# An expert stage with four row buffers each way, gathers four experts ahead, and down products one expert behind

## The reference

```python
def run_block(args):
    idx, e, w = args
    xb = x_pad[idx]
    hb = jax.nn.silu(xb @ w_gate[e]) * (xb @ w_up[e])
    return (hb @ w_down[e]) * w[:, None]
```

## Time and profile before

| | us |
|---|---|
| runs of the kernel, median of 3 | 1197.54 (1194.24 to 1198.41) |
| the profiled execution | 1196.28 |
| its span, first to last instruction | 1194.5 |
| mean granted clock of TensorE | 0.916 of full |

### The profile page before, as it was taken

How to read it: one execution, slowest core, us unless ns; L and a number is a source line. 1 busy time by engine, 2 the same in 40 slices (tenths; PEclk the granted TensorE clock), 3 DMA queues, 4 the chain that set the end, 5 groups by cost and what they waited for, 6 DMA issues and landing times.

```text
span 1194.5 us, 12870 instructions
## 1 busy us (share of the span) xinstructions
PE 1012.9 (85%) x4516; PEld 669.6 (56%) x4516; DVE 435.5 (36%) x952; ACT 297.3 (25%) x481; POOL 206.0 (17%) x376
## 2 busy tenths in 40 slices
PE   6699899999989979999999999758676768777596
PEld 6478677677867756666666644624333334333242
DVE  5595457339337632622232112321111111111443
ACT  3223432433433243311211100111111111111232
POOL 0131411330250121000000000033333333332000
PEclk9999899989979978999999999579888898888798
DMA  5221032022003022422222070616888888987401
GB/s 199 88 71 36 1 123 71 1 88 88 18 0 123 0 80 79 197 103 80 79 79 79 3 297 35 282 12 260 355 346 366 348 357 329 370 354 276 165 28 43
DMA packets 29071, 176.36 MB, mean 148 GB/s; under 512 B 11836, under 2 KB 12220, under 8 KB 22768
## 3 DMA queue, kind: packets, MB, share of 16 engines
q1 hardware_dynamic: 23600, 167.41, 36.1%
q0 software_dynamic: 5440, 8.54, 1.9%
HBM read 171.59 MB, written 12.71 MB: 154 GB/s over the span
## 4 chain that ended last, share of the span: by engine, by line
PE 55%; issue 22%; DVE 9%; POOL 6%; DMA 5%; ACT 2%; POOLq 1%; DVEq 0%; SPq 0%; ACTq 0%
PE bank L753 52%; DVE arena L1231 2%; DMA expert_rows<-mT,sidx 2%; POOL mT L1585 2%; DVE low_parts L1164 2%; POOL takes_wait L1577 2%; DMA mT<-normed,gidx 1%; DVE arena L1271 1%; DMA arena<-in_w_branch 1%; POOL expert_rows L1594 1%; PE bank L973 1%; PE bank L845 1%; DVE hT_parts L1159 0%; PE bank L781 0%; DMA x_sb<-in_x 0%
## 5 line engine op out<-in xcount | busy, mean ns | idle before, releaser
L753 PE MATMUL bank<-arena 128*128 128x64 f32 (+7 forms) x624 | 188.0, 454 | 23.1 <-DVE arena L1255 8.9
L753 PE MATMUL bank<-arena,yT 128*64 128x256 f32 (+1 forms) x1280 | 188.7, 452 | 12.7 <-ACT yT L703 11.8
L753 PE MATMUL bank<-mT_parts,low_parts 128*128 128x512 f32 x448 | 178.2, 398 | 0.0
L753 PEld LDWEIGHTS bank<-arena 128*128 128x128 f32 (+1 forms) x624 | 109.7, 217 | 97.6 <-issue 70.3
L753 PE MATMUL bank<-mT_parts,x_parts 128*128 128x512 f32 x320 | 138.7, 433 | 17.2 <-DVE low_parts L1164 13.5
L753 PEld LDWEIGHTS bank<-arena,yT 128*64 128x64 f32 x1280 | 93.3, 144 | 101.2 <-issue 49.3
L753 PE MATMUL bank<-hT_parts,x_parts 128*128 128x512 f32 x320 | 128.7, 402 | 0.0
L1164 DVE TENSOR_TENSOR low_parts<-arena,x_parts 128x1024 fp32r<-128x1024 f32 (+1 forms) x44 | 62.3, 1416 | 148.2 <-ACT x_parts L567 118.4
L753 PEld LDWEIGHTS bank<-mT_parts,low_parts 128*128 128x128 f32 x448 | 85.2, 190 | 20.0
L1022 PE MATMUL bank<-cst,mT 128*128 128x128 f32 x128 | 25.6, 333 | 74.2 <-DMA mT<-normed,gidx 74.2
L753 PE MATMUL bank<-yT,arena 128*128 128x512 f32 x192 | 86.3, 592 | 0.0
(11 more groups left out here) (227 smaller groups left out, 1209.2 us busy)
## 6 DMA issues: line engine op xcount, KB each, us to landing
arena<-in_w_expert SPq DMA_DIRECT2D x32, 3072.0 KB
arena<-in_w_cm SPq DMA_DIRECT2D x32, 512.0 KB, 3.6
arena<-in_w_gate SPq DMA_DIRECT2D x8, 1536.0 KB, 6.5
arena<-in_w_tm SPq DMA_DIRECT2D x4, 1536.0 KB, 6.7
arena<-in_w_branch SPq DMA_DIRECT2D x8, 768.0 KB, 7.9
x_sb<-in_x SPq DMA_DIRECT2D x8, 512.0 KB, 5.5
arena<-in_w_out SPq DMA_DIRECT2D x1, 4096.0 KB, 12.1
arena<-in_w_pg SPq DMA_DIRECT2D x2, 2048.0 KB, 9.5
```

Of the source, the lines that this page charges most:

```text
L753: return pe.matmul(out, lhsT, rhs, start=start, stop=stop)
```

## The change

- There are four gathered-row buffers and four scattered-row buffers (`ROWS = 4`) in place of two and two, each with its own semaphore. The memset ahead of the stage covers four row buffers, 2048 columns in place of 1024. VectorE's code and SyncE's are as before.
- GpSimd gathers the first four blocks at once; afterwards gather n + 4 is issued once block n is turned, still ahead of the wait for the scaled result of n and scatter n in the same queue. The indices are read by the indirect DMA straight from `table`: the copies, their waits and `take_wait` are gone from the main path. The loops of GpSimd and ScalarE are straight-line code.
- TensorE's step n is now up(n + 1), turning of the hidden block of n, turning of the rows of n + 2, down(n); up(0) and the turning of block 1 stand ahead of step 0. ScalarE's is sigmoid(n + 1), hidden copy(n), scaling(n).
- A weight buffer is still released by down(n), which now stands behind up(n + 1).

```diff
+ROWS = 4
...
-        xr = [mflat[:, b * 512:(b + 1) * 512] for b in range(2)]
-        yr = [mflat[:, (2 + b) * 512:(3 + b) * 512] for b in range(2)]
+        xr = [mflat[:, b * 512:(b + 1) * 512] for b in range(ROWS)]
+        yr = [mflat[:, (ROWS + b) * 512:(ROWS + b + 1) * 512] for b in range(ROWS)]
...
-            def scale_rows(n, b2, scattered):
+            def scale_rows(n, b2, slot, scattered):
                 act.wait_ge(down_done, n + 1)
-                act.wait_ge(rows_scattered[b2], scattered)
-                act.activation(yr[b2], Y[b2][:, :], ACT.Copy, scale=table_w(n)).then_inc(y_scaled, 1)
+                if scattered is not None:
+                    act.wait_ge(rows_scattered[slot], scattered)
+                act.activation(yr[slot], Y[b2][:, :], ACT.Copy, scale=table_w(n)).then_inc(y_scaled, 1)
             act.wait_ge(table_loaded, 32)
             act.wait_ge(routed, 2)
             n_over = act.value_load(ctl[0:1, 0:1], min_val=0, max_val=MAX_OVER)
-            with act.Fori(0, NEXP // RING) as i:
-                for b in range(RING):
-                    gate_sigmoid(RING * i + b, b % 2)
-                    hidden_copy(RING * i + b, b % 2)
-                    scale_rows(RING * i + b, b % 2, (1 + 2 * i + b // 2) * 16)
-            for b in range(2):
+            gate_sigmoid(0, 0)
+            for n in range(NEXP):
+                if n + 1 < NEXP:
+                    gate_sigmoid(n + 1, (n + 1) % 2)
+                hidden_copy(n, n % 2)
+                scale_rows(n, n % 2, n % ROWS, n // ROWS * 16 if n >= ROWS else None)
...
+            pe.wait_ge(we_loaded[0], 16)
+            up(0, 0, we[0], nothing)
+            turn_block(1, 1, rows_gathered[1], 16)
+
+            def expert_step(n, i, b, first=False, y_unused=False, last_one=False, before_last=False):
                 b2, other = b % 2, (b + 1) % 2
-                pe.wait_ge(we_loaded[b], (i + 1) * 16)
-                up(n, b2, we[b], nothing if gu_unused else lambda: pe.wait_ge(h_swished, n - 1))
                 if not last_one:
-                    turn_block(n + 1, other, rows_gathered[other], (2 * i + (b + 1) // 2 + 1) * 16)
+                    pe.wait_ge(we_loaded[(b + 1) % RING], (i + 1 + (b + 1) // RING) * 16)
+                    up(n + 1, other, we[(b + 1) % RING],
+                       nothing if first else lambda: pe.wait_ge(h_swished, n))
                 turn_hidden(n, b2)
-                down(n, b2, we[b], nothing if gu_unused else lambda: pe.wait_ge(y_scaled, n - 1))
+                if not last_one and not before_last:
+                    turn_block(n + 2, (b + 2) % ROWS, rows_gathered[(b + 2) % ROWS], (i + (b + 2) // ROWS + 1) * 16)
+                down(n, b2, we[b], nothing if y_unused else lambda: pe.wait_ge(y_scaled, n - 1))
             for b in range(RING):
-                expert_step(b, 0, b, gu_unused=b < 2)
+                expert_step(b, 0, b, first=b == 0, y_unused=b < 2)
...
-            pool.memset(mflat[:, 0:D], 0.0).then_inc(ready, 1)
+            pool.memset(mflat[:, 0:ROWS * 512], 0.0).then_inc(ready, 1)
...
-            def gather(b2, col, done, count):
-
-                take_wait(0)
-                pool.tensor_copy(gidx[:, b2:b2 + 1, :], table[:, bass.ds(col, 1), 0:2]).then_inc(idx_copied, 1)
-                pool.wait_ge(idx_copied, count + 1)
-                take_wait(1)
-                pool.indirect_dma_start(out=xr[b2], out_offset=None, in_=normed_halves,
-                                        in_offset=bass.IndirectOffsetOnAxis(ap=gidx[:, b2, 0:1], axis=0),
+            def gather_rows(slot, token_halves, done):
+
+                pool.indirect_dma_start(out=xr[slot], out_offset=None, in_=normed_halves,
+                                        in_offset=bass.IndirectOffsetOnAxis(ap=token_halves, axis=0),
                                         bounds_check=2 * SEQ - 1, oob_is_err=False).then_inc(done, 16)
-            def scatter(b2, col, done, count):
-                take_wait(0)
-                pool.tensor_copy(sidx[:, b2:b2 + 1, :], table[:, bass.ds(col, 1), 0:2]).then_inc(idx_copied, 1)
-                pool.wait_ge(idx_copied, count + 1)
-                take_wait(1)
+            def scatter_rows(slot, row_halves, done):
+
                 pool.indirect_dma_start(out=expert_halves,
-                                        out_offset=bass.IndirectOffsetOnAxis(ap=sidx[:, b2, 1:2], axis=0),
-                                        in_=yr[b2], in_offset=None, bounds_check=4 * SEQ - 1,
+                                        out_offset=bass.IndirectOffsetOnAxis(ap=row_halves, axis=0),
+                                        in_=yr[slot], in_offset=None, bounds_check=4 * SEQ - 1,
                                         oob_is_err=False).then_inc(done, 16)
-            gather(0, 0, rows_gathered[0], 0)
-            gather(1, 1, rows_gathered[1], 1)
+            for n in range(ROWS):
+                gather_rows(n, table[:, n, 0:1], rows_gathered[n])
             pool.wait_ge(routed, 2)
             n_over = pool.value_load(ctl[0:1, 0:1], min_val=0, max_val=MAX_OVER)
-            def serve(n, b2, gathers, scattered):
-
-                if gathers is not None:
+            for n in range(NEXP):
+                slot = n % ROWS
+                if n + ROWS < NEXP:
                     pool.wait_ge(rows_turned, n + 1)
-                    pool.wait_ge(rows_gathered[b2], gathers)
-                    gather(b2, n + 2, rows_gathered[b2], 2 + 2 * n)
+                    gather_rows(slot, table[:, n + ROWS, 0:1], rows_gathered[slot])
                 pool.wait_ge(y_scaled, n + 1)
-                pool.wait_ge(rows_scattered[b2], scattered)
-                scatter(b2, n, rows_scattered[b2], NEXP + n if gathers is None else 3 + 2 * n)
-
-            with pool.Fori(0, NEXP // RING - 1) as i:
-                for b in range(RING):
-                    serve(RING * i + b, b % 2, (2 * i + b // 2 + 1) * 16, (1 + 2 * i + b // 2) * 16)
-            for n in range(NEXP - RING, NEXP):
-                serve(n, n % 2, (n // 2 + 1) * 16 if n + 2 < NEXP else None, (1 + n // 2) * 16)
-            for b in range(2):
-                pool.wait_ge(rows_gathered[b], NEXP // 2 * 16)
+                scatter_rows(slot, table[:, n, 1:2], rows_scattered[slot])
```

More of the change, by code:

```diff
@@ L399, in build @@
         idx_copied = sem("idx_copied")
-        rows_gathered = [sem("rows_gathered0"), sem("rows_gathered1")]
+        blank_stored = sem("blank_stored")
+        rows_gathered = [sem(f"rows_gathered{b}") for b in range(ROWS)]
         rows_turned = sem("rows_turned")
@@ L410, in build @@
         y_scaled = sem("y_scaled")
-        rows_scattered = [sem("rows_scattered0"), sem("rows_scattered1")]
+        rows_scattered = [sem(f"rows_scattered{b}") for b in range(ROWS)]
         ov_w = sem("ov_w")
@@ L433, in build @@
         TM_AFTER, TM_TILE_AT = 4, 10
-        SCATTERED = (1 + NEXP // 2) * 16
+        SCATTERED = NEXP // ROWS * 16
         CM_ORDER = 8
@@ L713, in _ @@
             n_over = act.value_load(ctl[0:1, 0:1], min_val=0, max_val=MAX_OVER)
-            with act.Fori(0, NEXP // RING) as i:
-                for b in range(RING):
-                    gate_sigmoid(RING * i + b, b % 2)
-                    hidden_copy(RING * i + b, b % 2)
-                    scale_rows(RING * i + b, b % 2, (1 + 2 * i + b // 2) * 16)
-            for b in range(2):
+            gate_sigmoid(0, 0)
[4 more added lines that the diff above has]
+                scale_rows(n, n % 2, n % ROWS, n // ROWS * 16 if n >= ROWS else None)
+            for b in range(ROWS):
                 act.wait_ge(rows_scattered[b], SCATTERED)
@@ L725, in _ @@
                         hidden_copy(NEXP + j, 0)
-                        scale_rows(NEXP + j, 0, SCATTERED + j * 16)
+                        scale_rows(NEXP + j, 0, 0, SCATTERED + j * 16)
             for t in range(T):
@@ L1013, in _, with turn_block @@
                 ple(t)
-            def turn_block(n, b2, gathered, value, first=False):
+            def turn_block(n, slot, gathered, value, first=False):
                 pe.wait_ge(gathered, value)
@@ L1021, in turn_block @@
                 for k in range(KD // 2):
-                    last = pe.transpose(TR[:, k * P:(k + 1) * P], xr[b2][:, k * P:(k + 1) * P], ident)
+                    last = pe.transpose(TR[:, k * P:(k + 1) * P], xr[slot][:, k * P:(k + 1) * P], ident)
                 last.then_inc(rows_turned, 1)
@@ L1525, in _ @@
                 pool.dma_start(table_dram.rearrange("(j b) w -> j b w", b=NBLK)[slots], blank[slots, :, :])\
-                    .then_inc(rows_scattered[half], 16)
-            for half in range(2):
-                pool.wait_ge(rows_scattered[half], 16)
+                    .then_inc(blank_stored, 16)
+            pool.wait_ge(blank_stored, 32)
             pool.wait_ge(if_projected, T)
@@ L1616, in _ @@
-            for n in range(NEXP - RING, NEXP):
```

(21 more changed lines are left out.)

3 lines of the change are left out of this document (1 added, 2 removed).

## The result

The changed kernel takes 1154.97 us (median of 4 runs, 1151.8 to 1157.76) against 1196.51 us for the kernel before. The ratio is 0.9653, with a 95% interval of 0.9622 to 0.9684: 3.5% faster. The forecast was 1154.

What follows compares the result with a forecast made beforehand. The bound was taken as a loop: late gather, no buffer release, dry weight queue. The stage's end moving from 1108.25 to 1066.9 (41.4 us) plus 0.5 bookkeeping, off 1196.3, gave 1154 us; range 1142 to 1168.

Steps and rivals of the forecast that it cites:

- DMA bounds after the change, at 8.1 us an expert: Expert stage: loads, gathers and scatters, 3.41 MB an expert, set the pace at 8.1 us, above TensorE's own work.
- The start, 3.8 us lost: Start of the expert stage: up(1) now precedes down(0), so the weight stream begins at 820.2 us, 3.8 us later.
- the 0.5 us for GpSimd's bookkeeping: Gathers and last scatter: without index copies, GpSimd's issue work shrinks by 0.5 us at each end, bounds 0 and 1.15.
- TensorE's floor, 6.5 us: Expert stage: TensorE's own work at full clock, with its small gaps covered by the new order, takes 6.5 us an expert.
- Rows at 9.0 us an expert beside 24 KB packets: Expert stage: row transfers advance packet for packet with weights, so a scatter with a gather needs 9.0 us an expert.
- rival A: Expert stage: no gather limit, weights alone set the pace; 50.7 us off, 1146 us, or 1140 at 7.9 a load; chance 0.18.
- One dry spell of 2.5 us at 951: Expert stage, step 16: the weight queue runs dry from 951.3 to 953.8 us, and the gathers catch up meanwhile.
- Rival D, the clock: Expert stage: short TensorE stops in every expert lower its clock; slower, about 1214 us at 65% low-clock work; chance 0.05.
- Rival C, an HBM limit near 358 GB/s: Expert stage: HBM sustains only some 357 GB/s, 9.5 us a load; 11.5 us off, 1185 us; chance 0.05.

Runs made afterwards that it cites:

- e8: The changed kernel with 28 of the 32 expert weight loads cut from 24 to 20 KB a partition; 1119.47 us, ratio 0.9353.
- e4: The changed kernel with each expert's weights loaded by two DMAs (16 KB and 8 KB a partition) instead of one; 1153.44 us, ratio 0.9644.
- e1: The changed kernel with two row buffers each way instead of four, so gathers run two experts ahead; 1363.78 us, ratio 1.1391.

## Why the prediction was right, point by point

- **DMA bounds after the change, at 8.1 us an expert.** Right, and e8 with e4 shows it: 35.2 us for 14.7 MB less, with 34.6 expected. From the first full window to the end the share is about 1.0 at 417 GB/s on average.
- **The start, 3.8 us lost.** Right: 4.0 (S 130.2 against 126.2), with the first release at 820.1 us (820.2 forecast). Of the 0.5 us for GpSimd's bookkeeping some 0.4 are seen: the last scatter starts 0.77 us after ScalarE's end, where it started 1.20 us after it before.
- **TensorE's floor, 6.5 us.** Too high, at no cost: with everything at hand the step is 6.02 us (817.96 to 823.98).
- **Rows at 9.0 us an expert beside 24 KB packets.** The mechanism is right: the first wait for rows inside the stage came at step 4 (block 6, turned at 844.7 us), as forecast, gathers and weights alternate as the last waits, and splitting the loads removes the waits for rows altogether.
- **The price of that limit, the 8 us between 1154 and rival A's 1146.** This is the step that failed. With the limit gone (e4) the time was the same within the intervals. What was mis-sized is the volume term under it. TensorE's last up product in e4:

```profile
1053.02 3.67 PE L758 MATMUL bank<-arena,yT 128*64 128x256 f32 x32 [1.47 <-DMA arena<-in_w_expert]
```

  Its weights arrived 365.4 us after the first issue of weights, which is 1055.3 us on the changed kernel's time axis; rival A had 1048.8. From 821.7 us that makes 8.3 us a load and not 8.1. The mean rate of 418 GB/s gives 8.15, 1.4 of the 6.5 us. Most of the others show in the packets of the trace: a load has landed only when its last packet has, and by then the queue has gone on to the other weight behind it. In e4, 107 packets of 16 KB more than the experts' own start before the last packet of expert 31 ends: 1.75 MB, or 4.2 us at 418 GB/s. In the changed kernel there are 56, or 2.2 us, ahead of the end at 1052.5 us. The forecast had nothing for this. And the limit itself cost less than I took: it held TensorE at about 9 us a step (853.6 to 889.5 us) only until the rows caught up. They did so next to thin spots in the weight stream, as at 1009 us (columns as above):

```profile
1008.00:1010.00 2.00, 2.00 (x20) 1.16 (x18) 0.00 (x0) 0.69 (x1) 0.00 (x0) 1.00 0.88 271
1010.00:1012.00 2.00, 2.00 (x20) 1.09 (x16) 0.00 (x0) 0.00 (x0) 1.54 (x2) 1.00 0.74 273
```

  The two spots lose about 1 us in all (shares of 0.97 over 924 to 932 us and 0.87 over 1006 to 1012 us). So block 31 was turned at 1051.0 us, not 1054.6, and the end came at 1064.1, not 1066.9. The stage is 43.9 us shorter (E) where the forecast took 41.4, and that the median of all runs still lies within 1 us of 1154 is in part luck.
- **One dry spell of 2.5 us at 951.** Wrong in place and size; there were two thin spots, near 927 and 1009 us.
- **Rival D, the clock.** Its mechanism is seen: of the nine stops for rows of 1.9 us and over inside the stage, seven are followed by down and up in 6.5 to 7.1 us instead of 5.4. Inside the stage TensorE waits again for rows or weights behind most of these steps, so the 1.7 us should cost little there; no run measures it. Behind the last wait, at 1051.0 us, TensorE waits for no transfer any more, and the 7.08 us in place of 5.4 add 1.7 us to the end. In e1, where DMA idles, the low clock cost some 2 us in the step shown.
- **Rival C, an HBM limit near 358 GB/s.** Refuted: 417 GB/s over 220 us. The figure of the Trainium skill, DMA: Bandwidth & Descriptors, Specifications (about 358 GB/s for a core), did not hold for this kernel on one core; the measurement decides. The ceiling for the fabric in the same section, 435 GB/s, lies above the 427 GB/s of the fullest 30 us window, so the trace agrees with it.

Where the gain comes from is thus known. DMA was idle for 15% of 292 us, some 44 us. In the changed kernel the same stretch, 816 to 1064 us, has a share of 0.97 at 403 GB/s: 7 us idle, 4 of them the later start. That is 36 us less of idle time. The other 8 of the 44 us are busy time: the same 100 MB moved at 415 GB/s while busy (403/0.97) where it had been 404 (343/0.85). The order with down products one behind is not needed for it, and can't stand without the four buffers.

## What to carry to other kernels

When an engine waits for a small transfer that queues beside large ones, look at what the wait holds back: here it held back the release of weight buffers, and the idle DMA behind it was the loss, not the wait. Before a second limit is priced, ask what stands right behind it: taking it away is worth only the distance to the next, and two limits this close must be removed together (split loads alone or an early start alone brought nothing that could be measured, both together 4 to 8 us). Release a buffer in the parts in which it is read.

## What the runs showed of the hardware

- With the packets of rows (up to 4 KB) and of weights (24 KB) in flight together, the two queues advanced packet for packet (215 against 208 from 889 to 901 us). Cutting the weights' rows to 16 and 8 KB took TensorE's waits for rows, beyond the first, from 31.2 to 0 us, at the same rate of bytes (417 and 418 GB/s over 824 to 1044 us).
- Weights and rows together held 416 to 418 GB/s over 824 to 1044 us on one core (changed kernel twice, and e4).
- A load of 3 MB had landed only after packets of the load behind it had started: 56 of 16 KB in the changed kernel, 107 in e4, worth 2.2 and 4.2 us.
- TensorE's waits of 1.9 to 3.0 us were followed by a lower granted clock in some steps and not in others: after the wait of 2.0 us that ended at 853.6 us the next 40 matmuls took 7.1 us, after the 2.8 us that ended at 889.5 us they took 5.4.
